# Two-block transformer kernel: opening with six shift columns as TensorE products, sums of squares moved into the joint waits

## The chip, the cores and the metric

The kernel runs on one core of one Trainium2 chip, in float32. The metric is the device time of one execution in microseconds (us), lower is better. TensorE (PE) multiplies, its weight loads are shown apart (PEld); VectorE is DVE, ScalarE is ACT, GpSimd is POOL, SyncE (SP) issues most DMAs.

## The reference

The input is one sequence of 512 tokens by 1024 features. Two blocks are computed one behind the other. What the change touches is the start of the first one and the norms:

```python
c_act = jax.nn.silu(c)
for layer in range(2):
    mod = c_act @ ada_w[layer] + ada_b[layer]            # [1024] x [1024, 6*1024]
    sh1, sc1, g1, sh2, sc2, g2 = jnp.split(mod, 6, axis=-1)
    hn = rms_norm(h, norm1_g[layer]) * (1 + sc1) + sh1
    y = recurrent_mixer(hn, ...)      # layer 0: hn @ w_in, conv, gates, scan, @ w_out
                                      # layer 1: chunk attention on keys of shared_kv
    h = h + g1 * y
    hn = rms_norm(h, norm2_g[layer]) * (1 + sc2) + sh2
    h = h + g2 * (relu(hn @ w1) ** 2 @ w2)
def rms_norm(x, g): return x * lax.rsqrt(mean(x * x, -1) + 1e-6) * g
```

The second block (two layers of three gated attention branches, an output projection with a norm behind it and a side input) follows with the same rms_norm.

## The kernel before

Features lie on partitions: `h` is 8 tiles of 128 features x 512 tokens. All weights come as a stream of "units" of 8 blocks of 128x128 (512 KB), loaded by SP into two buffers `raw`. Each unit is split in two parts, `wh` (ACT, L212) and `wl` = raw - wh (DVE, L215), and each block costs three TensorE passes of 512 columns: wl x high, wh x low, wh x high (`mm3`, L220 to L222). Activations are split the same way (`xh`, `xl`). A full unit is 24 passes. Each engine runs one in-order list; `done` and `need` are semaphore events. A unit's `wh` may be written when the unit two before it is through (same buffer).

**The opening** (L595 to L700). SP loads `crow` (the vector c on all partitions), four pairs of tiles of x, `cst` (identity and ones), `vec` (all small vectors), then 16 tiles of modulation weights, 128 features x 1024 each, in the order scale 0, shift 0, scale 1, shift 1 and so on (`early_cols`), with the first two weight units behind the fourth and the sixth. ACT squares the 8 tiles of x (L618); PE sums them over the features with eight 512-column products against `ones` (L625), once `vec` and `cst` are in; ACT takes the root (L629), DVE the reciprocal over 128x512 (L654). For tile k, DVE makes two dot products of 1024 elements with c_act (`ada_dot`, L276: scale and shift), the gain (L664) and the shift (L667) from them, and h x 1/rms (L656); ACT applies gain and shift (L674) and rounds to `xh` (L677); POOL makes `xl` (L680); PE runs the four passes on `xh` for the first two units (L511, L512) and the two on `xl` (L516). This is `first_pair`. Behind the tiles ACT makes exp and log of lambda (L682, L684), each with a table load. Then `split_first` (L528, L531) makes the first halves of units 2 and 3.

After that, the recurrent layer: per j two units (conv and gate branches), DVE taps, dots for further modulation columns, gate units. Then the out projection (L900 on): 11 units. ACT issues four loads of modulation weights ahead of it, behind the event of the last gate (`G10v`). `rounded`, `recur` and `roots_of` of tiles 8 to 10 run in its first units.

**Norms** (`rstd_of`, L431). The squares of tiles 0 to 6 are added up on DVE while the last unit still runs; in the middle of that unit, `part_sums` sums them over the partitions with four single-column products (`token_sums`, L412; a float32 product shows as two records, so 8). Behind the unit, in the wait for the last tile's square, PE runs unused passes (`idle_passes`, L406) or other work (`between`), then the sums of the last tile, then ACT's root, DVE's reciprocal of 128x4, and a product that spreads it over all partitions (L458). This stands at seven places: M0n, KV and M1n (with unused passes, `norm_mod`), twice behind the second block's output projection ("z", with two `side` products), and twice at the start of the second block's layers, where value products stand in the wait.

**Keys** (`head_sums`, L1213): the sum of squares per head of key tile j is taken by PE behind unit j + 1, except tile 0, whose sum stands ahead of unit 2.

## Time and profile before

| what | us |
|---|---|
| median of 3 runs | 2553.05 (2550.53 to 2553.19) |
| the profiled execution | 2553.41, its span 2551.6 |
| PE busy | 2490.4 (98%), 12185 passes |
| DVE, ACT, POOL busy | 1443.1, 1125.9, 43.6 |
| from the start to the first pass of unit 2 | 60.85 |

The span is the time from the first to the last instruction on the chip; what lies around it in the profiled execution is 1.8 us. Busy times of PE come from modelled ends. The granted clock is TensorE's: 1.00 is 2.4 GHz and 0.50 is 1.2 GHz.

### The profile page before, as it was taken

Reading aid. Unit: us, or ns where it says so; the run is one execution under the profiler, and the core shown is the slowest. Engines: PE = TensorE matmul, PEld = TensorE weight load, DVE = VectorE, ACT = ScalarE, POOL = GpSimd, SP = SyncE. Lnnn points to the kernel's source line nnn. Section 1 sums busy time; section 2 is a strip of 40 time slices with the busy share of each in tenths; the row PEclk is TensorE's granted clock in tenths of the full one; section 3 lists DMA queues with packets and bytes.
Section 4 is the critical chain, followed back from the end, with each engine's and each line's share of the span. In section 5 each row is a group of like instructions: output and inputs, shape, how many; then the busy total and the mean of one; then the engine's idle time right before and its main releaser. Section 6 shows DMA issues by size and latency. Waiting matters only on the chain.

```text
span 2551.6 us, 32618 instructions
## 1 busy us (share of the span) xinstructions
PE 2490.4 (98%) x12185; PEld 1974.0 (77%) x12185; DVE 1443.1 (57%) x2237; ACT 1125.9 (44%) x1993; POOL 43.6 (2%) x28
## 2 busy tenths in 40 slices
PE   5999999999999999999999999999999999999998
PEld 2887888888777688888877777778877777777887
DVE  6987655556767653433456644554465664445445
ACT  4566433433546543433445534442354544443343
POOL 2000000000000000000000000000010000000001
PEclk7999999999999999999999999999999999999999
DMA  6633466666222123222231221222322121222223
GB/s 255 233 104 132 142 204 203 209 199 216 80 91 67 44 92 106 99 99 92 98 108 66 67 67 63 78 76 91 108 82 100 67 75 60 68 77 78 91 99 107
DMA packets 77901, 280.35 MB, mean 110 GB/s; under 512 B 8640, under 2 KB 8896, under 8 KB 77504
## 3 DMA queue, kind: packets, MB, share of 16 engines
q1 hardware_dynamic: 61056, 219.60, 25.5%
q10 hardware_dynamic: 16704, 58.79, 7.0%
q8 instruction: 98, 1.61, 0.3%
q14 instruction: 43, 0.35, 0.0%
HBM read 276.26 MB, written 2.10 MB: 109 GB/s over the span
## 4 chain that ended last, share of the span: by engine, by line
PE 93%; DVE 4%; ACT 2%; issue 1%; DMA 0%; ACTq 0%; SPq 0%; DVEq 0%
PE ps L220 27%; PE ps L222 25%; PE ps L221 25%; PE ps L1784 2%; PE ps L1871 2%; PE ps L1844 1%; PE ps L1687 1%; PE ps L1788 1%; PE ps L1180 1%; PE ps L1744 1%; PE ps L1107 1%; DVE wl L215 1%; PE ps L1160 1%; ACT wh L212 1%; PE ps L1968 1%
## 5 line engine op out<-in xcount | busy, mean ns | idle before, releaser
L215 DVE TENSOR_TENSOR wl<-raw,wh 128x1024 fp32r<-128x1024 f32 x374 | 459.1, 1227 | 651.2 <-ACT wh L212 651.0
L220 PE MATMUL ps<-xh,wl 128*128 128x512 f32 x1744 | 697.9, 400 | 9.6 <-DVE wl L215 3.5
L222 PE MATMUL ps<-xh,wh 128*128 128x512 f32 x1744 | 681.9, 391 | 0.0
L221 PE MATMUL ps<-xl,wh 128*128 128x512 f32 x1744 | 681.3, 391 | 0.0
L212 ACT ACTIVATE wh<-raw 128x1024 fp32r<-128x1024 f32 x374 | 394.9, 1056 | 632.4 <-PE ps L222 620.5
L220 PE MATMUL ps<-bh,wl 128*128 128x512 f32 x1174 | 464.9, 396 | 6.4 <-DVE wl L215 2.5
L222 PE MATMUL ps<-bh,wh 128*128 128x512 f32 x1174 | 458.0, 390 | 0.0
L221 PE MATMUL ps<-bl,wh 128*128 128x512 f32 x1174 | 457.6, 390 | 0.0
L220 PEld LDWEIGHTS ps<-xh,wl 128*128 128x128 f32 x1744 | 328.3, 188 | 127.6 <-issue 45.9
L222 PEld LDWEIGHTS ps<-xh,wh 128*128 128x128 f32 x1744 | 328.4, 188 | 70.5
L221 PEld LDWEIGHTS ps<-xl,wh 128*128 128x128 f32 x1744 | 328.8, 189 | 65.8 <-issue 1.4
L220 PEld LDWEIGHTS ps<-bh,wl 128*128 128x128 f32 x1174 | 220.9, 188 | 61.6 <-DVE wl L215 5.5
L222 PEld LDWEIGHTS ps<-bh,wh 128*128 128x128 f32 x1174 | 220.7, 188 | 46.9
L221 PEld LDWEIGHTS ps<-bl,wh 128*128 128x128 f32 x1174 | 221.0, 188 | 45.1 <-issue 1.0
L1026 DVE SCALAR_TENSOR_TENSOR h<-ps,mod,h 128x512 f32<-128x512 f32 x64 | 48.0, 751 | 136.4 <-PE ps L222 136.4
L276 DVE SCALAR_TENSOR_TENSOR bA<-bA,crow 128x1024 f32<-128x1024 f32 x74 | 89.6, 1220 | 4.8 <-DMA bA<-in_ada 4.8
L1828 ACT ACTIVATE bD<-ps,sm,crow 128x128 f32<-128x128 f32 (+3 forms) x64 | 39.0, 614 | 86.9 <-DVE sm L1808 86.9
L2442 POOL TENSOR_TENSOR xl<-h,xh 128x512 fp32r<-128x512 f32 x14 | 24.9, 1792 | 2424.6 <-ACT xh L2439 2424.6
L1707 ACT ACTIVATE bD<-bD,sm 128x128 f32<-128x128 f32 (+3 forms) x64 | 36.0, 563 | 62.0 <-DVE sm L1700 61.8
L1830 ACT ACTIVATE bD<-bD,sm 128x256 f32<-128x256 f32 (+1 forms) x64 | 30.3, 475 | 74.3 <-DVE sm L1814 74.3
L1044 DVE TENSOR_TENSOR bl<-bS,bh 128x512 fp32r<-128x512 f32 x64 | 44.2, 690 | 19.8 <-ACT bh L1021 19.8
L1625 ACT ACTIVATE bT<-ps 128x512 f32<-128x512 f32 x36 | 21.5, 597 | 76.3 <-PE ps L222 76.3
(314 smaller groups left out, 2540.4 us busy)
## 6 DMA issues: line engine op xcount, KB each, us to landing
raw<-in_w SPq DMA_DIRECT2D x388, 512.0 KB, 3.3
bA<-in_ada ACTq DMA_DIRECT2D x74, 512.0 KB, 4.6
bC<-in_ada SPq DMA_DIRECT2D x9, 512.0 KB, 10.9
bD<-in_ada ACTq DMA_DIRECT2D x8, 512.0 KB, 4.3
bS<-in_attn_bias ACTq DMA_DIRECT2D x8, 512.0 KB, 3.3
bD<-in_ada SPq DMA_DIRECT2D x7, 512.0 KB, 14.8
bC<-in_ada ACTq DMA_DIRECT2D x6, 512.0 KB, 3.8
h<-in_x SPq DMA_DIRECT2D x4, 512.0 KB, 6.4
```

Source lines behind the costliest of these rows:

```text
L212: e.activation(wh[p][:], raw[p][:], ACT.Copy).then_inc(s_hi, 1)
L215: e.tensor_tensor(wl[p][:], raw[p][:], wh[p][:].bitcast(F32), ALU.subtract)\
L220: e.matmul(out, wl[p][:, blk, 0:M], xhi, start=start, stop=False)
L221: e.matmul(out, wh[p][:, blk, 0:M], xlo, start=False, stop=False)
L222: return e.matmul(out, wh[p][:, blk, 0:M], xhi, start=False, stop=stop)
L276: return e.scalar_tensor_tensor(buf, buf, 0.5, crow[:], ALU.mult, ALU.mult, accum_out=dst)
L1026: e.scalar_tensor_tensor(h[:, m, :], ps[bk][:], mod[:, g2 + m:g2 + m + 1], h[:, m, :], ALU.mult, ALU.add).then_inc(s_bank[bk], 1)
L1044: done(e.tensor_tensor(bl[:, n, :], bS[:, 2 + q, :], bh[:, n, :].bitcast(F32), ALU.subtract), f"{ev}lo{n}")
L1707: done(e.activation(x, x, ACT.Exp, bias=nm(n, m), accum_out=rs(n, m)), f"{s}{n}ex{m}")
L1784: mm = e.matmul(out[m], st["q"][m], st["k"][m], start=True, stop=not st["low"])
L1828: i = e.activation(row(n, m), ps[2 + m][:, 0:nk], ACT.Exp, bias=nm(n, m), scale=st["scale"], accum_out=rs(n, m))
L1871: mm = e.matmul(ps[6 + n // NT % 2][HD * m:HD * m + HD, at:at + P], st["v"][m][b], x[:, P * b:P * b + P], start=b == 0, stop=b == st["nk"] ...
```

## The change

In words:

1. **Sums and products of the opening.** Squares of x are added in pairs on DVE, and PE sums four pairs over the partitions with single-column products into four banks, three unused passes behind each; sixteen unused passes on zeroed data stand ahead of them. Root and reciprocal are of 4 columns and not of 512, and a product spreads them.
2. **Six of the eight shift columns** (all but tiles 3 and 6) become products on PE: eight float32 products of one column, with the modulation weights as the stationary operand (the host turns those six tiles) and c_act as a column. Products 0 and 1 stand ahead of `first_pair`; product k + 2 stands in it between the passes on `xh` and on `xl` of tile k. The scale dots stay on DVE.
3. **Engines.** Gain and shift go from DVE to ACT; `xl` and the first two `wl` go from POOL to DVE. `cst` and `vec` are loaded earlier, shift comes before scale, and the two weight units behind the second tile. Exp and log of lambda move to `decay`, in the second step of the recurrent layer.
4. **Joint waits.** `part_sums` is gone; its products stand at the head of `rstd_of`, and at M0n, KV and M1n three unused passes follow and not six.
5. **Keys.** The head sum of tile 0 stands behind unit 2, with that of tile 1.
6. **Out projection.** ACT issues the four loads in its second unit and not ahead of the first.

```diff
+DOT_TILES = (3, 6)
...
-            def part_sums(s, n, sq):
-
-                def halfway(kt):
-
-                    if pe and kt == KD // 2:
-                        need(f"{s}sp{n - 2}")
-                        done(token_sums(sq(n - 2), 6), s + "part")
-                return halfway
 
...
                 if pe:
+                    need(f"{s}sp{n - 2}")
+                    done(token_sums(sq(n - 2), 6), s + "part")
                     between[0]()
...
+            def first_pair(u0, used, s, hi, lo, tiles=range(KD), between=lambda kt: None):
...
                             e.matmul(ps[q][:], wl[p][:, kt, :], hi[:, kt, :], start=kt == 0, stop=False)
                             e.matmul(ps[q][:], wh[p][:, kt, :], hi[:, kt, :], start=False, stop=False)
+                        between(kt)
                         need(f"{s}lo{kt}")
...
-            early_cols = [c for k in range(KD) for c in (KD + k, k)]
+            early_cols = [c for k in range(KD) for c in (k, KD + k)]
...
+                e.dma_start(cst[:], io["cst"]).then_inc(s_cst, 16)
                 for i in range(4):
                     e.dma_start(h[:, 2 * i:2 * i + 2, :], io["x"][:, 2 * i:2 * i + 2, :]).then_inc(s_x[i], 16)
-                e.dma_start(cst[:], io["cst"]).then_inc(s_par, 16)
-                e.dma_start(vec[:], io["vec"]).then_inc(s_par, 16)
+                    if i == 1:
+                        e.dma_start(vec[:], io["vec"]).then_inc(s_par, 16)
                 for i, a in enumerate(early_cols):
                     if i >= ADA_SLOTS:
                         need(f"i_ada{i - ADA_SLOTS}")
                     e.dma_start(early_slots[i % ADA_SLOTS], io["ada"][a]).then_inc(s_a0[i], 16)
-                    if i in (3, 5):
-                        e.dma_start(raw[i // 2 - 1][:], io["w"][i // 2 - 1]).then_inc(s_raw[i // 2 - 1], 16)
+                    if i == 1:
+                        for q in range(2):
+                            e.dma_start(raw[q][:], io["w"][q]).then_inc(s_raw[q], 16)
...
+                need("i_zero")
+                idle_passes(16)()
+                e.wait_ge(s_cst, 16)
+                for k in range(0, KD, 2):
+                    need(f"n0sp{k}")
+                    for t in range(NT):
+                        mm = e.matmul(ps[3 + t][:, 0:1], bT[:, k, P * t:P * t + P], ones[:, 0:1], start=k == 0, stop=k == KD - 2)
+                    if k == KD - 2:
+                        done(mm, "n0sum")
+                    idle_passes(3, 7)()
...
+            def shift_product(m):
+
+                if dve and m in DOT_TILES:
+                    e.wait_ge(s_a0[2 * m], 16)
+                    done(ada_dot(early_slots[2 * m % ADA_SLOTS], sm[:, SNM + KD + m:SNM + KD + m + 1]), f"i_ada{2 * m}")
+                if pe and m < KD and m not in DOT_TILES:
+                    if m == 0:
+                        need("i_cc")
+                    if m >= 4 and m - 4 not in DOT_TILES:
+                        need(f"n0sh{m - 4}")
+                    e.wait_ge(s_a0[2 * m], 16)
+                    for kt in range(KD):
+                        mm = e.matmul(ps[2 + m % 4][:, 0:1], early_slots[2 * m % ADA_SLOTS][:, P * kt:P * kt + P], c_col[:, kt:kt + 1],
+                                      start=kt == 0, stop=kt == KD - 1)
+                    done(mm, f"i_ada{2 * m}")
+
+            if pe:
+                idle_passes(2, 6)()
+                shift_product(0)
+                idle_passes(4, 6)()
+                shift_product(1)
...
-                        done(ada_dot(early_slots[i % ADA_SLOTS], sm[:, SNM + i:SNM + i + 1]), f"i_ada{i}")
+                    shift_product(k)
+                    if k:
+                        e.wait_ge(s_a0[2 * k + 1], 16)
+                        done(ada_dot(early_slots[(2 * k + 1) % ADA_SLOTS], sm[:, SNM + k:SNM + k + 1]), f"i_ada{2 * k + 1}")
+                    if 0 < k < KD - 1:
+                        done(e.tensor_tensor(bT[:, k + 1, :], h[:, k + 1, :], ps[7][:], ALU.mult), f"n0r{k + 1}")
...
-            first_pair(0, BK, "n0", xh, xl)
+            first_pair(0, BK, "n0", xh, xl, between=lambda kt: shift_product(kt + 2))
...
-            if act:
-                need(f"G{KW - 1}v")
-                for k in range(4):
-                    ada_load(2 * KD + N_EARLY + k, out_slots[k], k)
...
+                if act and j == 1:
+                    need(f"G{KW - 1}v")
+                    for k in range(4):
+                        ada_load(2 * KD + N_EARLY + k, out_slots[k], k)
...
-                    rstd_of(s, KD, D, bTk, (idle_passes(6), idle_passes(4)), lambda: split(U[0] + 1, 0, 0))
+                    rstd_of(s, KD, D, bTk, (idle_passes(3), idle_passes(4)), lambda: split(U[0] + 1, 0, 0))
...
-                if j:
-                    head_sums(j - 1)
+                if j > 1:
+                    for m in (0, 1) if j == 2 else (j - 1,):
+                        head_sums(m)
```

## Rows read from the trace of the kernel before

**Rows 1.** The chain that ended last, shares of the span by engine.

```profile
PE 93%; DVE 4%; ACT 2%; issue 1%; DMA 0%; ACTq 0%; SPq 0%; DVEq 0%
```

**Rows 2.** Stretches: us; PE, PEld, DVE, ACT, POOL busy; clock; DMA share; GB/s.

```profile
11.88:30.20 18.32, 9.78 (x16) 3.94 (x16) 13.21 (x19) 5.48 (x8) 4.65 (x3) 0.83 1.03 412
30.20:56.00 25.80, 17.48 (x42) 10.00 (x42) 24.70 (x42) 9.50 (x14) 12.56 (x7) 0.70 0.51 193
...
70.00:100.00 30.00, 30.00 (x134) 24.71 (x133) 28.04 (x43) 15.73 (x22) 0.00 (x0) 1.00 0.71 246
```

**Rows 3.** The chain in order of time: start, us, what.

```profile
3.57 8.26 DMA vec<-in_vec
11.88 9.79 PE ps L625 x16
```

**Rows 4.** Timeline of one input tile in the opening: start, us, instruction.

```profile
44.18 1.82 POOL L680 TENSOR_TENSOR xl<-bT,xh 128x512 fp32r<-128x512 f32 x1 [2.28 <-ACT xh L677]
...
44.80 1.22 DVE L664 SCALAR_TENSOR_TENSOR gs<-sm,mod,vec 128x1 f32<-128x1 f32 x1
...
46.02 0.68 DVE L656 TENSOR_TENSOR bT<-h,bT 128x512 f32<-128x512 f32 x1
...
46.73 0.81 ACT L674 ACTIVATE bT<-bT,mod,gs 128x512 f32<-128x512 f32 x1 [2.63 <-DVE bT L656]
...
47.57 0.63 ACT L677 ACTIVATE xh<-bT 128x512 fp32r<-128x512 f32 x1
...
48.91 1.22 DVE L664 SCALAR_TENSOR_TENSOR gs<-sm,mod,vec 128x1 f32<-128x1 f32 x1
```

**Rows 5.** Timeline where the opening hands over to unit 2.

```profile
59.46 1.13 ACT L528 ACTIVATE wh<-raw 128x512 fp32r<-128x512 f32 x2
...
60.85 0.79 PE L220 MATMUL ps<-xh,wl 128*128 128x512 f32 x1 [1.46 <-DVE wl L531]
...
62.72 0.33 PEld L222 LDWEIGHTS ps<-xh,wh 128*128 128x128 f32 x1
...
65.17 0.40 PE L221 MATMUL ps<-xl,wh 128*128 128x512 f32 x1
```

**Rows 6.** Two stretches late in the kernel, around single-column products.

```profile
2051.80:2055.20 3.40, 3.24 (x31) 3.16 (x28) 1.09 (x2) 2.62 (x5) 0.00 (x0) 0.97 0.00 0
2055.20:2062.00 6.80, 5.23 (x21) 4.57 (x21) 2.39 (x9) 3.60 (x11) 0.00 (x0) 0.51 0.24 77
```

**Rows 7.** Timeline right after: products of 128 columns at the low clock.

```profile
2056.77 1.11 PE L1728 MATMUL ps<-cst,bD 128*128 128x128 f32 x4 [1.73 <-DVE bD L1720]
```

**Rows 8.** Timeline, the out projection's last unit and the first joint wait.

```profile
276.79 1.08 PEld L412 LDWEIGHTS ps<-cst,bT 128*128 128x128 f32 x8
...
282.36 1.05 PE L412 MATMUL ps<-cst,bT 128*128 128x1 f32 x8
...
284.28 1.15 PE L458 MATMUL ps<-cst,sm 128*128 128x128 f32 x8
```

**Rows 9.** Timeline, joint wait behind the second block's output projection.

```profile
1854.15 1.16 PE L458 MATMUL ps<-cst,sm 128*128 128x128 f32 x8 [0.49 <-DVE sm L453]
```

**Rows 10.** Timeline, key tiles: first head sum and unit 2.

```profile
655.73 1.13 PE L1219 MATMUL ps<-bT,cst 128*128 128x512 f32 x2 [1.53 <-ACT bT L1261]
...
656.92 0.39 PE L221 MATMUL ps<-xl,wh 128*128 128x512 f32 x1
```

**Rows 11.** Timeline at the start of the out projection.

```profile
225.92 1.06 ACT L212 ACTIVATE wh<-raw 128x1024 fp32r<-128x1024 f32 x1 [2.48 <-issue]
...
228.29 0.50 PE L220 MATMUL ps<-bh,wl 128*128 128x512 f32 x1 [2.31 <-DVE wl L215]
...
228.96 0.69 DVE L804 TENSOR_TENSOR bD<-bD,bA 128x512 f32<-128x512 f32 x1 [0.72 <-ACT bA L797]
...
233.28 1.23 DVE L215 TENSOR_TENSOR wl<-raw,wh 128x1024 fp32r<-128x1024 f32 x1 [0.26 <-ACT wh L212]
...
235.49 0.39 PE L220 MATMUL ps<-bh,wl 128*128 128x512 f32 x1
```

More of the change, by code:

```diff
@@ L498, in normed @@
                 put_lo(s, n - 1, y, shift, hi, lo)
-            def first_pair(u0, used, s, hi, lo, tiles=range(KD)):
+            def first_pair(u0, used, s, hi, lo, tiles=range(KD), between=lambda kt: None):
                 if pe:
@@ L618, in program @@
                     done(e.activation(bT[:, k, :], h[:, k, :], ACT.Square), f"n0sq{k}")
-                e.wait_ge(s_par, 32)
+                e.wait_ge(s_par, 16)
+                done(e.activation(c_th, v("c", 0, KD), ACT.Tanh, scale=0.5), "i_cth")
                 done(e.activation(sm[:, 62:63], v("eps"), ACT.Sqrt), "n0tb")
-            if pe:
-                e.wait_ge(s_par, 32)
-                for k in range(KD):
-                    need(f"n0sq{k}")
-                    mm = e.matmul(ps[7][:], ones, bT[:, k, :], start=k == 0, stop=k == KD - 1)
-                done(mm, "n0sum")
+            root = sm[:, 0:NT]
@@ L628, in program @@
                 need("n0sum")
-                done(e.activation(bT[:, 8, :], ps[7][:], ACT.Sqrt, scale=1.0 / D, bias=v("eps")), "n0root")
+                for t in range(NT):
+                    i = e.activation(root[:, t:t + 1], ps[3 + t][:, 0:1], ACT.Sqrt, scale=1.0 / D, bias=v("eps"))
+                done(i, "n0root")
+            if dve:
+                e.wait_ge(s_a0[1], 16)
+                done(ada_dot(early_slots[1], sm[:, SNM:SNM + 1]), "i_ada1")
+                need("n0root")
+                done(e.reciprocal(root, root), "n0inv")
@@ new lines, in program @@
+            if pe:
+                need("n0inv")
+                for t in range(NT):
+                    mm = e.matmul(ps[7][:, P * t:P * t + P], root[:, t:t + 1].to_broadcast([P, P]), ident, start=True, stop=True)
+                done(mm, "n0rstd")
+            def shift_product(m):
[4 more added lines that the diff above has]
+                    if m == 0:
+                        need("i_cc")
+                    if m >= 4 and m - 4 not in DOT_TILES:
[5 more added lines that the diff above has]
+                    done(mm, f"i_ada{2 * m}")
@@ L632, in program @@
                     e.activation(wh[q][:], raw[q][:], ACT.Copy).then_inc(s_hi, 1)
-            if pool:
+            if dve:
+                need("n0rstd")
+                for m in range(2):
+                    done(e.tensor_tensor(bT[:, m, :], h[:, m, :], ps[7][:], ALU.mult), f"n0r{m}")
                 for q in range(2):
@@ L679, in program @@
+                if dve:
+                    for m in (k - 1,) if 0 < k < KD - 1 else (k - 1, k) if k else ():
                         need(f"n0hi{m}")
                         done(e.tensor_tensor(xl[:, m, :], bT[:, m, :], xh[:, m, :].bitcast(F32), ALU.subtract), f"n0lo{m}")
-            if act:
-                done(e.activation(sm[:, SLAM:SLAM + KW], v("lam", 0, KW), ACT.Exp, scale=-1.0), "i_el")
-                need("i_el")
-                done(e.activation(sm[:, SLAM:SLAM + KW], sm[:, SLAM:SLAM + KW], ACT.Ln, bias=ones[:, 0:1]), "i_sp")
@@ L686, in decay @@
             def decay():
+                if act:
+                    e.wait_ge(s_cst, 16)
+                    done(e.activation(sm[:, SLAM:SLAM + KW], v("lam", 0, KW), ACT.Exp, scale=-1.0), "i_el")
+                    need("i_el")
+                    done(e.activation(sm[:, SLAM:SLAM + KW], sm[:, SLAM:SLAM + KW], ACT.Ln, bias=ones[:, 0:1]), "i_sp")
                 if dve:
@@ L985, in mlp @@
                         elif not up:
-                            unit_pe(u0, 0, i, [(bk, used, *FULL, (bh, bl))], before=by_tile(ev) if n == KD else
-                                    part_sums(nxt, KD, bTk) if c == N_FF - 1 and n == 2 * KD - 1 else None)
+                            unit_pe(u0, 0, i, [(bk, used, *FULL, (bh, bl))], before=by_tile(ev) if n == KD else None)
                         def dots():
@@ L1442, in program @@
                 elif n > 1:
-                    unit_pe(u0, 0, n, [(bk, used, *FULL, (bh, bl))], before=part_sums("M1n", KD, bTk) if n == KD - 1 else None)
+                    unit_pe(u0, 0, n, [(bk, used, *FULL, (bh, bl))])
                 if act or dve:
@@ L2467, in program @@
                     if m > 1:
-                        unit_pe(u0, 0, m, [(bk, used, *FULL, (xh, xl))],
-                                before=part_sums("L1n", KD, bDk) if l == 0 and m == KD - 1 else None)
+                        unit_pe(u0, 0, m, [(bk, used, *FULL, (xh, xl))])
                     if act:
@@ L2685, in _vectors @@
         sinks=rows(a["sw_sinks_2"]), inv_freq=freq,
-        eps=np.full((P, 1), EPS, np.float32))
+        eps=np.full((P, 1), EPS, np.float32), c=_features(a["c"][0]))
     return np.ascontiguousarray(np.concatenate([parts[k] for k in VEC], 1))
@@ L2721 @@
     ada = np.ascontiguousarray(ada.reshape(N_ADA + 2, P, D))
+    for m in range(KD):
+        if m not in DOT_TILES:
+            ada[m] = ada[m].reshape(P, KD, P).transpose(2, 1, 0).reshape(P, D)
     cst = np.zeros((P, 4, P), np.float32)
```

79 lines of the change are left out of this document (39 added, 40 removed).

## The prediction

> **What bounds the kernel now.** I read the chain of waits first, by engine [rows 1]: PE carries 93% of it, so only what PE runs, or what it waits for, counts. Then I cut the span into stretches [rows 2]. From 70 us on PE has no idle time worth the name; in 70 to 100 it is busy for all 30 us, 134 passes of 512 columns at 0.224 each, with DVE at 28.04 of 30 beside it. Before that it is not: from 30.20 to 56.00 it ran 42 passes in 25.80 us at a mean clock of 0.70, and DVE is busy 24.70 of them. So the kernel is an opening of about 61 us set by DVE, and some 2490 us of passes with a few holes.
>
> In the opening the chain [rows 3] goes through the landing of `vec` at 11.83, which PE needed for nothing but its place in the queue, then 9.79 us of sums. The timeline of a tile [rows 4] shows the period: the gain L664 of one tile starts at 44.80, of the next at 48.91, so 4.11 us a tile. In it DVE has the gain, which takes 1.22 for one column and ends where POOL's 1.82 us (44.18 to 46.00) end, 0.68 for the product with h, and in what is left, 2.2, its two dots, 1.1 each. ACT's 0.81 and 0.63 and PE's six passes fit inside. At the end [rows 5] ACT starts the halves of unit 2 only at 59.46, behind its two table loads; unit 2 starts at 60.85, with passes 0.43 apart until 65.17, when 0.227 begins. Ten passes in 4.32 us where 2.27 would do: 2.05 us lost to the clock. At the full clock unit 2 would have had the same end had it started at 62.9.
>
> **The opening, changed.** The bytes ahead of the modulation weights are the same (crow, cst, x, vec), so the last x lands where `vec` landed, near 11.8. Two squares (under 0.81 each, an L674's price) and an addition put the last pair at 13.6. Four single-column products are 8 records; in the joint wait they take 1.05, and from their start to the end of the spreading product it is 3.1 us (282.36 to 285.43) [rows 8]. The opening has four roots in place of one there, but no addition: I take the same, so 1/rms is spread at 16.7 plus up to 1 for the three extra roots and the dot of scale 0 that stands in DVE's list: 17.7. Now PE's sums alone end at 21.7 [rows 3], and its first pass waits until 30.2 [rows 2].
>
> A shift product is 16 records, 1.05 for 8, so 2.1. Two passes and product 0 end at 20.3; ACT's bias and gain (one column each, put at 0.2, between nothing and L674's 0.81), then 0.81 and 0.63 give the first high half at 22.3. Four passes and product 1 hold PE until 23.3.
> From there DVE's list is the longest: two products with h and two `wl` (1.23 each, as L215 [rows 11]) end at 21.5; then seven scale dots and two shift dots (9.9), six products with h and eight lows at 0.68 (9.5), and about 2.4 of waiting for ACT at the first and the last tile: 43.3. PE has 48 passes at 0.227 (10.9) and four products (8.4), 19.3 from 23.3: it fits under DVE by a hair. The pair of tiles k and k + 2 on PE and ACT (0.9 of passes, 2.1, then ACT's 1.9 and 0.3 of semaphores) gives 5.2 for two, 2.6 a tile: also about 43. The half of unit 2, which no table load delays now, ends 0.7 behind the last low, at 44.0. All three limits meet, so I add 1.5 for what they do to each other: unit 2 starts at 45.5, at the full clock. Modulation tiles land 1.27 apart (512 KB at 412 GB/s [rows 2]), the last near 35, five us ahead of its dot; the weight loads of units 2 and 3, behind it in SP's list, are issued near 33 and needed at 42. **Gain 62.9 - 45.5 = 17.4.**
>
> What leaves POOL costs DVE 0.7 a tile, and the gain's wait for POOL (about 1.1) goes. Exp and log come back in the second step. Tile 5 is rounded at 48.20, so tile 7 two periods on, at 56.4 [rows 4], and ACT is free again at 59.46 [rows 5]: 3.0 us with two table loads. ACT is busy 15.73 of 30 us in the next stage [rows 2], so this lies beside PE's work; DVE, which waits for it, is busy 28.04. I count nothing, and keep up to 3 us for it as a rival.
>
> **Out projection.** ACT spent 2.48 us issuing DMAs, then rounded unit 2's weights at 225.92, and PE stood 2.31 us until 228.29, then ran slow, as 7.2 us for the 24 passes to 235.49 show, where 5.45 would do [rows 11]. With the loads behind, rounding starts 2.4 earlier and this hole closes. Late next is unit 3: its `wl` hangs on root, recurrence and rounding of tile 8, from 228.96 to 234.51, 5.55 us. With the first root about 2.5 earlier it is ready at 232.0; PE would want it at 225.8 + 5.45 = 231.3, so 0.7 of waiting is left. Unit 3 started at 235.49: **gain 3.4**. The four loads (some 1.9 us of ACT's time) then lie ahead of a rounding that waits for DVE anyway, and their first dot is three units on.
>
> **Joint waits.** Taking `part_sums` out of the last unit gives back 1.08 of weight loads less the 0.19 that would stand there, 0.9 [rows 8]. At M0n, KV and M1n the six passes that fill the wait are 1.4 at 0.227; 8 records and three passes are 1.7, and DVE and ACT need about as long for the last tile's update and square: **3 x 0.9 = 2.7**. At the two z places PE is idle for only 0.49 ahead of the spreading product [rows 9], with `side` work in both gaps: I take **2 x 0.5 = 1.0**. At the two layer starts value products fill the wait already, and the sums change place only: 0. Both ends: 0 and 0.9 a place.
>
> **Keys.** PE waits 1.53 for the first head sum, and from its start to the second pass of unit 2 it is 1.19 [rows 10]. Unit 2's first half is ready, so it starts at once; the sum costs 0.9 behind it. **Gain 1.8** (the wait and what comes with it).
>
> **Sum:** 17.4 + 3.4 + 2.7 + 1.0 + 1.8 = 26.3. From the profiled 2553.41, which is 0.36 over the median: 2527.1.
>
> **A price no row shows, and the clock.** A single-column product at the low clock is not in the trace. At the full clock a record is 0.13 [rows 8]; 128-column ones at the low clock are 1.11 for four, 0.28 [rows 7]. Between them I take 0.13, as I expect the clock up after sixteen unused passes in a row: at 65.17 it rose behind ten [rows 5]. But in 2051.80 to 2055.20 PE is busy 3.24 of 3.40 us, mostly with single-column products, and the clock is 0.51 in the stretch that follows [rows 6]: such products did not hold it. The Trainium skill, "TensorE: Matmul & The Clock Gate", Part 1, says the gate follows how busy the engine has lately been, idle being the low state; read by busy time it would hold 2.4 GHz through the whole opening and leave the first rival below without a chance. The row speaks the other way, so it keeps one.
>
> **Rivals.**
> *The clock falls in the opening.* In favour: the rows just read, and the mean of 0.70 from 30.20 to 56.00. Against: the unused passes, and that DVE's list, the longest, knows no clock. A low clock over half of the pair stage makes 24 passes dearer by 0.2 (4.8) and two products by up to 2.4 each: unit 2 at 51 to 53. With 52: 2533.6. **Chance 0.22.**
> *DVE keeps the next stage.* It is busy 28.04 of 30, and PE now comes 2 us earlier against it by the better clock. If all of it is given back, with the exp and log on top of it, 3 us: 2530. Against: PE did not wait once in that stretch. **0.13.**
> *The opening gains nothing:* the clock stays low all through. Unit 2 then starts near 46 + 96r for a record price r (96 records in six products; 48 passes at 0.43 are 20.5; 22.3 + 4 for the slower start, less 3.8 counted in r; 3 of waits). At 0.13 that is 58.5; unit 2 ran slow before too, so against 60.85: gain 2.4, and 8.9 elsewhere: 2542. At 0.20 it is 65.2 and the time 2548.9. **0.04.**
> *Slower:* the same place, with the loads of the products not hidden, 0.33 each as a load at the low clock [rows 5]. Unit 2 at 77.7, 16.8 late, less 8.9: 2561.3. The point from which it decides is unit 2 at 69.8, a record price of 0.25. **0.03.**
> *My forecast:* **0.58**, 2527.1, itself within 2522 and 2531.
>
> A measurement here can tell about 0.2%, 5.1 us. Faster by more: 0.94. Same: 0.03. Slower: 0.03. The range takes in forecast, the falling clock and the next stage: 2520 to 2538; its low end is every term at its best (unit 2 at 43.4, 0.9 at all seven waits: 2522.4) and the 2.7 us by which the runs before differ, in part.
>
> **What would show it.** Unit 2's first pass at 45.5 (43.4 to 53), passes 0.227 apart there; 1/rms spread near 17.7; a period of 2.6 to 3 us in the pair; L212 of the out projection's unit 2 at its old place less 2.4 and a hole of 0.7 one unit later; no single-column records inside last units; no wait ahead of the keys' unit 2. Wrong if the granted clock is 0.50 from 20 to 45, or if a product takes over 3 us.

## The result, and the profile after

The changed kernel ran in 2537.55 us, the median of 4 runs (2536.39 to 2540.88), beside 2553.12 for the kernel before (2550.53 to 2553.43): a ratio of 0.9943, 95% interval 0.9931 to 0.9955. That is 15.6 us of the 26.3 forecast, and the profiled execution (2536.39) lies 17.0 under the profiled one of before. Run once more in a later session, the same kernel had a median of 2532.01 in 6 runs (2530.81 to 2540.88), ratio 0.9923, 0.9907 to 0.9939. By the ratios the gain is 14.6 us (11.5 to 17.6) and 19.7 us (15.6 to 23.7): the forecast of 26.3 lies outside both, though 2537.55 is still inside the range of 2520 to 2538. Both measurements belong to the result, as will be seen.

The page of the changed kernel, its head and the chain of waits by engine:

```profile
span 2534.6 us, 32918 instructions
...
PE 93%; DVE 3%; ACT 2%; issue 1%; DMA 0%; ACTq 0%; SPq 0%; DVEq 0%
```

It looks as in [rows 1]. The opening doesn't. These are its stretches, in the columns of [rows 2], one behind the other:

```profile
9.10:12.40 3.30, 2.99 (x21) 2.41 (x20) 1.62 (x3) 2.56 (x6) 0.00 (x0) 1.00 1.01 395
12.50:22.70 10.20, 10.20 (x39) 9.08 (x38) 3.49 (x11) 5.10 (x11) 0.00 (x0) 0.50 1.02 413
22.80:26.10 3.30, 3.30 (x27) 3.12 (x27) 3.30 (x4) 1.36 (x4) 0.00 (x0) 1.00 1.02 405
26.20:36.30 10.10, 10.10 (x38) 9.04 (x38) 7.84 (x15) 5.18 (x12) 0.00 (x0) 0.50 1.00 400
36.40:46.00 9.60, 9.25 (x59) 7.95 (x58) 8.31 (x15) 6.25 (x13) 0.00 (x0) 1.00 0.59 222
```

PE is busy 10.20 of 10.20 us at a granted clock of 0.50 (1.2 GHz), has 3.30 us at 1.00 (2.4 GHz), and then 10.10 at 0.50 again. What that did to single instructions, in the timeline of PE (start, duration; L646 is a sum, L408 an unused pass, L663 the spreading, L678 a shift product, L506 at 27.95 the first pass of the pair, L222 unit 2):

```profile
14.06 1.70 PE L646 MATMUL ps<-cst,bT 128*128 128x1 f32 x8
15.62 1.63 PE L408 MATMUL ps<-bh 128*128 128x512 f32 x3
17.05 1.70 PE L646 MATMUL ps<-cst,bT 128*128 128x1 f32 x8
...
20.03 1.91 PE L663 MATMUL ps<-cst,sm 128*128 128x128 f32 x8
...
27.95 0.77 PE L506 MATMUL ps<-xh,wl 128*128 128x512 f32 x1
...
29.81 3.41 PE L678 MATMUL ps<-mod,bC 128*128 128x1 f32 x16
...
51.38 0.40 PE L222 MATMUL ps<-xh,wl 128*128 128x512 f32 x1
```

A sum is 1.70 where eight records had been 1.05 [rows 8], the three passes behind it 1.63 (0.94 at the full clock), and the last sum starts at 17.05 although its squares were added at 14.1. A product at the low clock is 3.41, 0.21 a record: the price no row had shown, between my ends of 0.13 and 0.28. Unit 2 starts at 51.38, not at 45.5.

Here is the same kernel, same instructions, in the execution profiled later:

```profile
12.50:22.70 10.20, 9.98 (x73) 8.98 (x73) 7.41 (x16) 7.41 (x15) 0.00 (x0) 1.00 1.03 413
...
26.20:36.30 10.10, 9.77 (x53) 8.27 (x52) 10.10 (x17) 6.20 (x13) 0.00 (x0) 0.83 1.03 409
```

```profile
14.74 0.95 PE L646 MATMUL ps<-cst,bT 128*128 128x1 f32 x8
...
16.71 1.16 PE L663 MATMUL ps<-cst,sm 128*128 128x128 f32 x8 [0.22 <-DVE sm L659]
...
22.59 0.47 PE L506 MATMUL ps<-xh,wl 128*128 128x512 f32 x1
...
23.60 1.84 PE L678 MATMUL ps<-mod,bC 128*128 128x1 f32 x16
...
45.26 0.40 PE L222 MATMUL ps<-xh,wl 128*128 128x512 f32 x1
```

The same 10.2 us held 73 records in place of 39, 1/rms was spread at 17.87 (forecast 17.7; 21.94 in the first trace), and unit 2 started at 45.26 (forecast 45.5). So unit 2 starts at 45 or at 51 us by what the clock does ahead of it, and 5.4 of the 6.1 us between the two are there before the pair begins (22.59 and 27.95). The times differ in the same way: ten executions of this kernel fall in two groups, four of 2530.8 to 2532.4 at mean clocks of 0.994 and 0.995, six of 2536.4 to 2540.9 at 0.989 to 0.992. The first measurement had four of the second group. One execution of each group was traced, 2530.81 and 2536.39; that the other eight had one of these two openings is likely, but no trace shows it.

**Where the time went, place by place.** I matched PE's passes of a trace with those of the kernel before in their order, and took the lead (start before less start after) on both sides of each place. For example, unit 2 of the out projection starts at 228.29 [rows 11] and at 216.52: a lead of 11.8.

| place (start before, us) | forecast | after | after, 2nd execution |
|---|---|---|---|
| opening (to 66) | 17.4 | 11.5 | 17.6 |
| next stage (66 to 100) | 0 | -2.2 | -2.2 |
| out projection (225 to 245) | 3.4 | 3.3 | 3.3 |
| joint wait M0n (270 to 290) | 0.9 | 0.6 | 0.6 |
| KV (625 to 645) | 0.9 | 0.9 | 1.0 |
| keys (655 to 670) | 1.8 | 1.8 | 1.8 |
| M1n (915 to 935) | 0.9 | 1.0 | 1.0 |
| layer start (1270 to 1290) | 0 | 0.1 | 0.1 |
| z (1840 to 1860) | 0.5 | 0.9 | 1.0 |
| layer start (1900 to 1950) | 0 | 1.0 | 0.9 |
| z (2475 to 2495) | 0.5 | 0.9 | 0.9 |
| clock elsewhere, and rest | 0 | -2.9 | -3.2 |
| **sum** | **26.3** | **17.0** | **22.8** |

The last line but one is a net figure: the kernel before has falls of its own in these stretches.

The next stage's rows (after): DVE goes from one instruction to the next without a break, and PE waits for its `wl`.

```profile
75.61 1.21 DVE L278 SCALAR_TENSOR_TENSOR bC<-bC,crow 128x1024 f32<-128x1024 f32 x1
...
76.75 1.22 DVE L217 TENSOR_TENSOR wl<-raw,wh 128x1024 fp32r<-128x1024 f32 x1
```

```profile
62.79 0.50 PE L222 MATMUL ps<-xh,wl 128*128 128x512 f32 x1 [0.33 <-DVE wl L217]
78.03 0.50 PE L222 MATMUL ps<-xh,wl 128*128 128x512 f32 x1 [1.34 <-DVE wl L217]
```

```profile
70.00:100.00 30.00, 28.66 (x127) 23.40 (x126) 28.50 (x43) 18.77 (x26) 0.00 (x0) 1.00 0.78 264
```

PE has 127 passes where it had 134 [rows 2]. DVE's first step of the stage is 9.2 us earlier than before (52.73 for 61.91) and its list was as long, so 9.2 is what PE can keep of its 11.5; in the second execution 15.4 of 17.6.

Out projection, unit 2 and the unit behind it (beside [rows 11]):

```profile
216.52 0.46 PE L222 MATMUL ps<-bh,wl 128*128 128x512 f32 x1
...
222.69 0.50 PE L222 MATMUL ps<-bh,wl 128*128 128x512 f32 x1 [0.48 <-DVE wl L217]
```

The hole of 2.31 is gone, and one of 0.48 (forecast 0.7) has come one unit later. The first joint wait (beside [rows 8]):

```profile
267.10 0.95 PE L414 MATMUL ps<-cst,bT 128*128 128x1 f32 x8
...
268.77 1.05 PE L414 MATMUL ps<-cst,bT 128*128 128x1 f32 x8
...
271.04 1.16 PE L453 MATMUL ps<-cst,sm 128*128 128x128 f32 x8 [0.18 <-DVE sm L448]
```

And a place where the clock fell in this trace but not in the one of before:

```profile
735.00:746.00 11.00, 9.83 (x45) 7.00 (x45) 7.69 (x16) 5.79 (x14) 0.00 (x0) 0.84 0.32 109
```

The stretch 751 to 762 of before has the same work at 1.00; here 1.5 us go. (In the traces of `best1`, `best2` and both with dots it did not fall there.) The next fall that the kernel before did not have, at 1852, takes the lead from 16.2 to 13.6. Behind 2495 it is the kernel before that loses more, and 1.2 come back. The second layer start brings 1.0 that I had put at 0, for a reason that stood in the trace of before and that I had not read: inside that last unit PE waited for the sum of squares.

```profile
1908.92 1.05 PE L412 MATMUL ps<-cst,bD 128*128 128x1 f32 x8 [0.82 <-DVE bD L399]
```

### The profile page after: what moved, and what is told of

The parts are those of the page before. It is cut to its first block, busy times and chain, and to the rows that moved or that the text cites. A ratio compares the mean times of both kernels' runs of the same rounds, so it can differ in the third digit from the quotient of the medians.

```text
span 2534.6 us, 32918 instructions
## 1 busy us (share of the span) xinstructions
PE 2503.8 (99%) x12330; PEld 1996.8 (79%) x12330; DVE 1433.1 (57%) x2225; ACT 1131.5 (45%) x2013; POOL 25.0 (1%) x18
## 4 chain that ended last, share of the span: by engine, by line
PE 93%; DVE 3%; ACT 2%; issue 1%; DMA 0%; ACTq 0%; SPq 0%; DVEq 0%
PE ps L222 26%; PE ps L224 25%; PE ps L223 25%; PE ps L1831 2%; PE ps L1918 2%; PE ps L1891 1%; PE ps L1734 1%; PE ps L1835 1%; DVE wl L217 1%; PE ps L1226 1%; PE ps L1791 1%; PE ps L1153 1%; ACT wh L214 1%; PE ps L1206 1%; PE ps L408 1%
## 5 line engine op out<-in xcount | busy, mean ns | idle before, releaser
L222 PE MATMUL ps<-xh,wl 128*128 128x512 f32 x1744 | 698.2, 400 | 9.8 <-DVE wl L217 5.2
L222 PE MATMUL ps<-bh,wl 128*128 128x512 f32 x1174 | 463.7, 395 | 4.4 <-DVE bl L1388 2.0
L222 PEld LDWEIGHTS ps<-xh,wl 128*128 128x128 f32 x1744 | 328.5, 188 | 127.7 <-issue 45.4
L222 PEld LDWEIGHTS ps<-bh,wl 128*128 128x128 f32 x1174 | 220.5, 188 | 59.9 <-issue 4.8
L1090 DVE TENSOR_TENSOR bl<-bS,bh 128x512 fp32r<-128x512 f32 x64 | 44.2, 690 | 19.8 <-ACT bh L1067 19.8
L1171 ACT ACTIVATE bA<-bA,sm 128x128 f32<-128x128 f32 (+3 forms) x64 | 36.0, 563 | 38.3 <-DVE sm L1165 35.0
```

The lines of the kernel that those rows point to most:

```text
L222: e.matmul(out, wl[p][:, blk, 0:M], xhi, start=start, stop=False)
L1090: done(e.tensor_tensor(bl[:, n, :], bS[:, 2 + q, :], bh[:, n, :].bitcast(F32), ALU.subtract), f"{ev}lo{n}")
```

## The experiments

The question: why 15.6 and not 26.3, and is it the clock, DVE's list or the products? Each kernel ran beside the kernel before, whose own 31 executions in these sessions were 2549.92 to 2557.27, so times are compared by ratio; a mean clock is rounded to 0.001, which is 2.5 us in one execution. "Work" below is the mean of time x granted clock, "clock" the rest of the mean time. It tells executions of one kernel apart; between kernels it is only a hint, as a low clock while PE waits is in it. Two ratios whose intervals overlap are not told apart by these times.

| kernel | ratio to before (95%) | median | lowest, highest | work + clock |
|---|---|---|---|---|
| changed, 10 executions | 0.9943 and 0.9923 | 2536.5 | 2530.8, 2540.9 | 2516.2 + 19.8 |
| opening_only | 0.9958 (0.9943 to 0.9972) | 2542.6 | 2538.7, 2547.7 | 2525.6 + 17.4 |
| later_only | 0.9961 (0.9948 to 0.9974) | 2545.1 | 2541.6, 2546.8 | 2518.4 + 26.0 |
| more_passes | 0.9920 (0.9907 to 0.9932) | 2533.6 | 2531.1, 2536.0 | 2521.3 + 12.2 |
| none_between | 0.9927 (0.9914 to 0.9941) | 2532.9 | 2530.8, 2539.8 | 2514.2 + 20.3 |
| dots_all | 0.9911 (0.9897 to 0.9924) | 2531.4 | 2528.8, 2536.8 | 2518.5 + 14.2 |
| dots_again | 0.9932 (0.9919 to 0.9945) | 2536.1 | 2533.1, 2541.8 | 2517.4 + 19.3 |
| short_dots | 0.9902 (0.9887 to 0.9917) | 2528.2 | 2527.2, 2533.3 | 2514.0 + 15.2 |
| best1 | 0.9909 (0.9893 to 0.9924) | 2530.6 | 2528.6, 2532.6 | 2515.4 + 15.2 |
| best2 | 0.9907 (0.9892 to 0.9922) | 2528.8 | 2527.5, 2534.6 | 2516.7 + 13.3 |
| best3 | 0.9897 (0.9883 to 0.9911) | 2528.7 | 2528.2, 2529.2 | 2518.0 + 10.7 |

**The opening alone, and the rest alone.** `later_only` is the kernel before with the places behind the opening changed, as in the cut below; `opening_only` is the changed kernel with all of them put back:

```diff
                 if pe:
+                    need(f"{s}sp{n - 2}")
+                    done(token_sums(sq(n - 2), 6), s + "part")
                     between[0]()
...
-                        if m == KD - 1:
-                            part_sums("M0n", KD, bTk)(kt - 3)
...
+                if act and j == 1:
+                    need(f"G{KW - 1}v")
+                    for k in range(4):
+                        ada_load(2 * KD + N_EARLY + k, out_slots[k], k)
...
-                    rstd_of(s, KD, D, bTk, (idle_passes(6), idle_passes(4)), lambda: split(U[0] + 1, 0, 0))
+                    rstd_of(s, KD, D, bTk, (idle_passes(3), idle_passes(4)), lambda: split(U[0] + 1, 0, 0))
...
-                if j:
-                    head_sums(j - 1)
+                if j > 1:
+                    for m in (0, 1) if j == 2 else (j - 1,):
+                        head_sums(m)
```

> The changed opening with all later parts as before. Ledger of the two traces: unit 2 of the first stage is 11.4 us earlier, of which 9.4 are left from 88 us on, when DVE has kept the next stage. So 2553.1 - 9.4 = 2543.7. Rival (the loss of 2 us in the next stage has nothing to do with the opening): 2541.7. Rival (opening as forecast, 17.4, and the trace of after was an unlucky one): 2535.7.

> The opening as before, the out projection's loads, the sums in the joint waits and the keys' head sum as changed. Ledger of the traces by place: 3.4 + 0.4 + 0.9 + 1.8 + 1.0 + about 0 at the layer starts and the z places = 7.5, so 2545.6. By the forecast's terms 8.9: 2544.2. Rival (the lead after the opening is what lets these gains come through, DVE would keep them otherwise): under 5, above 2548.

2542.6 and 2545.1, 10.0 and 7.5 under the 2552.6 of the kernel before beside them: both first theories, within 1.1 us. By the ratios they are 10.7 and 10.0, each within some 3.5 us, so the times alone show only roughly that the parts add up. The traces show more. In that of `later_only` the places of its theory give 3.3, 0.9, 1.0, 1.8 and 1.0, in the whole change 3.3, 0.6, 0.9, 1.8 and 1.0. But the z places and the second layer start, which the theory had at about 0, give 2.8 more, and falls of the clock elsewhere take back some 4 of the 10.9: that the median met 7.5 is luck. In that of `opening_only` unit 2 starts at 51.96, the next stage returns 2.2, and two places that it leaves alone move: the out projection gives 0.8, as a fall of the clock that the kernel before has at 229 us is missing, and M0n gives -0.35. So M0n leans on the opening: DVE's addition there starts 0.46 us behind the end of the last sum in every trace with tile 0's shift column as a product, and 0.10 behind it in every other. The reason stays open.

**More unused passes, and none between the sums.** `more_passes` and `none_between` against the changed kernel:

```diff
-                    idle_passes(3, 7)()
+                    idle_passes(6, 7)()
...
-                idle_passes(2, 6)()
+                idle_passes(6, 6)()
...
-                idle_passes(4, 6)()
+                idle_passes(8, 6)()
...
-            between=lambda kt: shift_product(kt + 2)
+            between=lambda kt: (idle_passes(4 if kt == 0 else 0, 6)(), shift_product(kt + 2))
```

```diff
-                    idle_passes(3, 7)()
+                    if k == KD - 2:
+                        idle_passes(3, 7)()
```

> Changed kernel with six unused passes behind each sum in place of three, six ahead of product 0 in place of two, eight between products 0 and 1 in place of four, and four ahead of product 2. Theory A (the clock set the opening's miss): the granted clock stays up from its first rise on, products 1.84 in place of 2.7 and 3.4, unit 2's first pass near 47 in place of 51.4, the time 2 to 4 us under the changed kernel's (the next stage returns up to half). Theory B (DVE's list and the order of the pair set it): unit 2 at 51 to 52 even with the clock up, no gain. If the clock falls all the same: unit 2 at 53 or later, slower than the changed kernel by 1 to 3.

> Changed kernel without the unused passes behind the first three sums (three stay behind the last). In the trace of after they did not hold the clock and stood in the sums' way, 1.63 us for three at the low clock. Theory A1 (they only cost): the last sum starts at 14.2 in place of 17.05, 1/rms is spread near 19.5 in place of 21.9, unit 2 near 49.5, time down by 1.5 to 2.5. Theory A2 (they give back what they cost, as the clock stays low longer without them): last sum at 14.2 all the same, but the low clock lasts through more of the pair and unit 2 comes at 51 to 54, time the same or up to 2 us more.

`more_passes`: the clock stayed up through the sums and the first four products and fell later in the pair. Its stretches and two instructions:

```profile
12.00:20.00 8.00, 8.00 (x50) 7.07 (x50) 3.14 (x10) 4.93 (x11) 0.00 (x0) 1.00 1.03 415
...
36.00:46.00 10.00, 10.00 (x38) 8.65 (x36) 6.71 (x11) 4.79 (x10) 0.00 (x0) 0.53 0.72 270
```

```profile
36.81 3.41 PE L678 MATMUL ps<-mod,bA 128*128 128x1 f32 x16
...
50.98 0.40 PE L222 MATMUL ps<-xh,wl 128*128 128x512 f32 x1
```

So A held only for the sums: unit 2 at 50.98 in this execution. The added passes have a price of their own, as the pair's first pass came at 25.80, 3.2 later than in the second execution of the changed kernel, with the clock up in both. Yet the highest of its five times is 2536.0, where six of the changed kernel's ten are above that. Its work is 5 us dearer, its clock 8 cheaper. `none_between` is the other way round: the last sum starts at 14.80, unit 2 at 49.55, A1 in this trace; its times lie in two groups (four of 2530.8 to 2533.8, two of 2539.2 and 2539.8), so A2 may be what two of the six executions did; no trace shows those.

**Products or dots.** All eight shift columns on DVE:

```diff
-DOT_TILES = (3, 6)
+DOT_TILES = tuple(range(8))
```

> Changed kernel with all eight shift columns as DVE dots (no product at all; the rest of the opening as changed). Products took 14.2 us of PE in the trace of after between 22.6 and 47.6; six dots are 6 x 1.22 more for DVE. Theory A (PE is the longest of the pair as the clock is low in it, DVE has room of about 3 us): DVE's list from 22 is 31 us, unit 2 at 53 to 54, time 2 to 3 us over the changed kernel's ratio. Theory B (DVE was the longest already): unit 2 at 58 to 59, 7 us over. If products were a loss: unit 2 before 51.4.

Unit 2 started at 53.36, the 53 to 54 of theory A, and PE waited for DVE's low halves once in each of five tiles, four times for 1.43 us:

```profile
47.51 0.73 PE L512 MATMUL ps<-xl,wh 128*128 128x512 f32 x2 [1.43 <-DVE xl L729]
...
53.36 0.39 PE L222 MATMUL ps<-xh,wl 128*128 128x512 f32 x1
```

But its median was 2531.4, 6 under the changed kernel's first one, against every theory. Before making a story of it I ran both kernels in turn on one chip.

> The changed kernel once more, beside two others. In the runs so far the time of an execution times its mean granted clock is nearly constant for one kernel (changed: 2515.9 with a spread of 0.4 in four runs; before: 2528.8), and what differs is what the clock takes: 20 to 25 us. Theory A (the clock falls at other places from one execution to the next, the work is the same): time times clock again 2515 to 2517, times between 2530 and 2541. Theory B (the changed kernel has a fixed clock pattern, two falls of 10 us in the opening each time): times within 2536 to 2541 as before, clock 0.990 to 0.992 in each.

> The kernel with all eight shift columns as dots once more, on the same chip and in turn with the changed one. If the products are what the clock falls over (theory A), it is faster than the changed kernel in the same session by 3 us or more, with a mean clock of 0.993 to 0.996, though its unit 2 starts 2 us later at the same clock. If its 2531.4 was only what the clock happened to do in five executions (theory B): within 2 us of the changed kernel, or slower by up to 2.

2532.0 for the changed kernel, 2536.1 for the dots. Theory A for the first, though time times clock went from 2512.6 to 2518.2 in single executions, beyond its band by more than the rounding of the clock. The second is not faster, so its theory A is out; it is slower by 4.1 by the medians and by 2.3 by the ratios, where B had up to 2. The 2531.4 was what five executions happened to give. At a low clock over the sums in all three, unit 2 starts at 53.4 and 53.7 with dots and at 51.4 with products: in the traces the six products are worth 2 us or a little more, as the low clock lasted to 36.4 us there and to 33.2 and 33.3 with dots. The times don't show that: the ratios overlap, and over ten executions each the means are 2534.7 with dots and 2535.9 with products.

**DVE in the next stage.**

```diff
-            def ada_dot(buf, dst):
-
-                return e.scalar_tensor_tensor(buf, buf, 0.5, crow[:], ALU.mult, ALU.mult, accum_out=dst)
+            def ada_dot(buf, dst, w=2 * T):
+
+                return e.scalar_tensor_tensor(buf[:, 0:w], buf[:, 0:w], 0.5, crow[:, 0:w], ALU.mult, ALU.mult, accum_out=dst)
...
-                        done(ada_dot(conv_slots[k], mod[:, 2 * KD + t:2 * KD + t + 1]), f"g1ada{t}")
+                        done(ada_dot(conv_slots[k], mod[:, 2 * KD + t:2 * KD + t + 1], 64 if t < 6 else 2 * T), f"g1ada{t}")
```

> Changed kernel with the first six modulation dots of the next stage over 64 columns in place of 1024 (their outputs are then other ones; it leaves out 6 x 1.1 us of DVE). Theory A (DVE keeps the next stage, and so returns 2 of the 11.4 us): PE's waits of 0.33 at 62.8 and 1.34 at 78.0 go, the lead on before stays at 11 us or more, time down by 1.7 to 2. Rival (the waits come from ACT's order, its exp, log and loads ahead of the rounding): the waits stay, no change.

This kernel leaves out most of six dots, so its output is another one; it serves for its times alone.

```profile
71.19 0.43 PE L222 MATMUL ps<-xh,wl 128*128 128x512 f32 x1
```

This is the pass that waited 1.34 at 78.03; it waits for nothing now, though PE is earlier (unit 2 at 46.69). The lead over before is 16.2 at 66 us and 16.2 at 100 us: nothing is returned. In the changed kernel PE's waits there were 1.7 us, and 2.2 were returned. Theory A. The time, 2528.2, has the lowest work of all kernels, 2514.0. The opening is that of the changed kernel, and the clock in it took a third course:

```profile
12.00:20.00 8.00, 7.78 (x55) 6.92 (x56) 5.16 (x12) 5.51 (x12) 0.00 (x0) 1.00 1.03 415
20.00:26.00 6.00, 6.00 (x30) 5.47 (x29) 5.97 (x10) 3.84 (x8) 0.00 (x0) 0.64 1.03 408
26.00:36.00 10.00, 10.00 (x47) 8.81 (x47) 7.77 (x14) 5.10 (x11) 0.00 (x0) 0.70 1.02 405
```

It was up over the sums and low over the start of the pair, and unit 2 was only 1.4 us later than at its best.

**Six passes kept in the joint waits.**

```diff
-                    rstd_of(s, KD, D, bTk, (idle_passes(3), idle_passes(4)), lambda: split(U[0] + 1, 0, 0))
+                    rstd_of(s, KD, D, bTk, (idle_passes(6), idle_passes(4)), lambda: split(U[0] + 1, 0, 0))
```

> Changed kernel with six unused passes in the joint waits as in the kernel before, in place of three. Read at the places alone, from the lead over the kernel before ahead of the sums to that behind the spreading product: 0.44 at the first, 0.94 and 1.0 at the next two in the changed kernel. If the three passes taken out are what was gained: 0.7 less at each of the three. If DVE's and ACT's work for the last tile sets the wait: no difference, and the gain is that of the records alone.

By the leads: 0.1, 0.5 and 0.5 at M0n, KV and M1n in place of 0.6, 0.9 and 1.0. So about 0.5 of each gain is the three passes, where the first theory had 0.7, and the rest is the records. This is one execution; in the other traces KV and M1n are 0.9 to 1.0 throughout, M0n is 0.6 in the five with tile 0's shift column as a product and 0.9 to 1.0 in the other six.

**Another opening.** The diff is that of `best1`, but for its last two lines: these are what `best2` adds to it, three passes behind each product in the pair but tile 7's; `best3` has 38, 6 and 12 unused passes for 32, 5 and 5, and column 1 among the dots, so that product 1 goes.

```diff
-DOT_TILES = (3, 6)
+DOT_TILES = (0, 3, 6)
...
+                    if k in (2, 4):
+                        need(f"n0sp{k}")
+                        done(e.tensor_tensor(bT[:, k, :], bT[:, k, :], bT[:, k - 2, :], ALU.add), f"n0st{k}")
+                        need(f"n0st{k}")
...
-                idle_passes(16)()
+                idle_passes(32)()
...
-                for k in range(0, KD, 2):
+                for k in (4, 6):
...
-                    idle_passes(3, 7)()
+                    if k == KD - 2:
+                        idle_passes(5, 7)()
...
+                e.wait_ge(s_a0[0], 16)
+                done(ada_dot(early_slots[0], sm[:, SNM + KD:SNM + KD + 1]), "i_ada0")
+                need("n0root")
+                done(e.reciprocal(root, root), "n0inv")
...
-                idle_passes(2, 6)()
-                shift_product(0)
-                idle_passes(4, 6)()
-                shift_product(1)
+                idle_passes(5, 6)()
+                shift_product(1)
...
-            between=lambda kt: shift_product(kt + 2)
+            between=lambda kt: (shift_product(kt + 2), idle_passes(3 if kt + 2 < KD and kt + 2 not in DOT_TILES else 0, 6)())
```

> Changed kernel with another opening: squares of tiles 0 to 5 added up on DVE, so two sums in place of four; 32 unused passes ahead of them, none between, five behind; shift column 0 as a DVE dot ahead of the reciprocal, the scale column 0 behind it; product 1 alone ahead of the pair. Spread near 16.5 to 17.5 in place of 21.9, first pass of the pair near 20.5 in place of 27.95. Then DVE's list of 23 us: unit 2 at 44 to 46 if the clock stays up, and the lead of the first conv step over before grows by as much: 2531. If the clock falls in the pair, as it did with products and passes alone: unit 2 at 48, 2534. Rival (the modulation tiles' landing or DVE's next stage keeps it all): 2537.

> As best1, with three unused passes behind each of the three products in the pair that come before tile 7's, and that one. They cost 0.7 each on PE. Theory A (the clock falls in the pair because of the products, and passes behind them hold it): no low stretch before unit 2, unit 2 at 43.5 to 45.5, at or under best1's time. Rival (PE's order is the longest even at the full clock, the passes only cost): unit 2 up to 2.5 us later than best1's.

> As best2, with shift column 1 as a DVE dot too, so that nothing but 512-column passes, one pair of sums and the spreading product runs ahead of the pair: 38 unused passes ahead of the sums, six behind, twelve behind the spreading. DVE's list is longer by 1.2 us. Theory A (holding the clock is worth more than a dot): clock up from its first rise to the end of the opening, unit 2 at 45 to 46.5, mean clock 0.996, time 2527 to 2529. Rival (DVE's list sets the pair once the clock is up): unit 2 at 47 or later, 2530 or more.

```profile
45.31 0.51 PE L222 MATMUL ps<-xh,wl 128*128 128x512 f32 x1 [1.15 <-DVE wl L527]
```

```profile
24.56 3.41 PE L685 MATMUL ps<-mod,bC 128*128 128x1 f32 x16
...
47.62 0.39 PE L222 MATMUL ps<-xh,wl 128*128 128x512 f32 x1
```

The first is `best1`, the second `best2`. Both medians lie under both of the changed kernel's, but their ratios overlap with its second one. In both traces the clock fell once behind the sums and once in the pair, and `best1` came out at its forecast of 2531 all the same. In `best2` it fell before its first three passes behind a product (24 to 31 us), so passes behind products were not tested there; unit 2 was 2.3 later than in `best1`, as its rival had it, but with the clock low for longer, so that this decides nothing between the two. In `best3` it did not fall in the opening, nor until 732 us:

```profile
9.00:45.00 36.00, 34.46 (x191) 28.46 (x190) 31.15 (x54) 24.87 (x50) 0.00 (x0) 1.00 0.97 389
```

```profile
23.57 1.84 PE L685 MATMUL ps<-mod,bC 128*128 128x1 f32 x16
...
45.10 0.50 PE L222 MATMUL ps<-xh,wl 128*128 128x512 f32 x1
```

Its four times lie within 1.0 us of each other, where every other kernel that was run more than once spread over 4 to 10. Theory A: 2528.7, the lowest ratio of the table, 3.3 under the changed kernel's median in the same session and 9 under the first measurement; its interval just overlaps with that of the changed kernel's second one. Its lowest time is within 1.1 us of those of `short_dots`, `best1` and `best2`; what it didn't have, in four executions, are long ones. It differs from `best2` in three counts of passes and in product 1, so which of them kept the clock up is open, and so is whether four executions are enough to say that it stays up.

## Why the prediction was wrong

**The parts, with the clock up over the sums, were right.** In the second execution, where the clock fell only for short stretches in the pair, the opening gave 17.6 (17.4), the out projection 3.3 (3.4), the keys 1.8 (1.8), the five joint waits 4.4 (3.7). The spread 1/rms, unit 2's start and the new hole of the out projection came within 0.3 us. Of the seven waits, M0n was put too high (0.6 for 0.9, by 0.35 that the changed opening costs there), both z too low (0.9 for 0.5), and the second layer start gave 1.0 where I had said 0; without the next stage the places of this execution sum to 28.2, for 26.3.

**First step that failed: the forecast took the sum of every term at a clock that holds, and priced its fall as a rival of 0.22.** "I expect the clock up after sixteen unused passes in a row." It is up by their end, from 9.1 on, but it does not hold: it is at 0.50 from 12.5 and again from 26.2, the opening's term of 17.4 measured 11.5, and six executions of ten took 7.5 us more than the other four (means of 2539.0 and 2531.4). Five traces have this very opening: two of the changed kernel, `opening_only`, `short_dots` and `six_kept`. In two the clock fell over the sums (at 12.5 and 13.2 us): 1/rms was spread at 21.9 and 22.5, unit 2 started at 51.4 and 52.0, and the gain at 66 us was 11.5 and 10.9. In three it fell later (at 21.7, 22.0 and 30.6): 1/rms at 17.7 to 17.9, unit 2 at 45.3 to 46.9, the gain 16.0 to 17.6. So it is a low clock over the sums that costs. The rival had unit 2 at 51 to 53, and it came at 51.38, but that is in good part luck: I had put the loss in the pair, where even the low stretch of `short_dots` cost only 1.4 us. Over the sums it costs twice, as the unused passes stand in the sums' way, 1.63 us for three. The row that I had read against the change, PE busy 3.24 of 3.40 us with single-column products and then 0.51 [rows 6], was the better witness than the three unused passes between.

The Trainium skill, "TensorE: Matmul & The Clock Gate", Part 1, has the gate follow how busy the engine has been. Read by the busy time of the profile, the traces here don't agree: in 12.50 to 22.70 PE was busy for all 10.20 us at 0.50, and in the other execution for 9.98 at 1.00; and in the two stretches ahead of the falls, 9.10 to 12.40 and 22.80 to 26.10, it was busy 2.99 and 3.30 of 3.30 us at 1.00. `best3`, with 38 passes in a row and passes behind its products, is the only opening in which no fall was seen.

**Second step that failed: the next stage, "I count nothing".** The rival of 0.13, priced at 3 us, came every time: 2.1 to 2.4 us are returned in every trace of a changed opening with the dots at full length, and none in `short_dots`. The rows had it: DVE at 28.04 of 30 beside a PE that did not wait once [rows 2]. What I argued from, that PE did not wait, was true only while PE was as late as DVE; the 2.05 us that the better clock gives unit 2 are PE's alone, and DVE returns just these. The exp and log cost nothing on top: `short_dots` has them too and returns nothing.

**Third: rivals that can hold together were given as alternatives.** The clock and DVE's list both took their part, and with a net 2.9 us for the clock outside the opening (falls at 740 and 1852 us of the trace above all; I had counted none) the sum for the profiled run is 26.3 - 5.9 (opening) - 2.2 (next stage) - 2.9 (clock elsewhere) + 1.7 (the small places) = 17.0. The range reached to 2538 and held six of the ten executions of the changed kernel (2530.8 to 2536.6); it lacked what one kernel's executions differ by, 10 us.

**The other rivals.** The clock low all through, or a product's records above 0.25: neither; records are 0.21 at the low clock, and the clock was never low from 20 to 45 without a break. No run tests their tipping points. Of the two signs of being wrong that I had named, one came: a product took over 3 us (3.41 at 29.81). It is no special price of a product, only the low clock.

What stays open: why the clock falls over the sums in one execution and not in the next, with the same instructions. In the first it rose at about 9, in the second at about 7, but that does not sort them: of the five traces with this opening it rose first in that of `opening_only`, at 6.4, and fell over the sums there. Nor was it tried to hold the clock at 740 or 1850.

## What to carry to other kernels

Where PE's work is thin, first ask in how many executions the clock holds: compare the granted clocks of several runs, not of one profile, since the same kernel may differ by 10 us. Then ask where a low clock would lie on the path: over a chain that everything waits for (here the sums) it cost 4 to 5 us, over a stretch that DVE's list covers 1 to 2. If such a chain depends on it, cover it with 512-column passes while PE waits for others anyway, and keep single-column products out of it: in `best3`, the kernel that went furthest in this, the long executions were missing. Passes where PE does not wait cost what they take. And when PE gets ahead, look for the engine that was exactly as late: what it can't follow is given back at its next long list.

## What the runs showed of the hardware

- Single-column products: 16 records take 1.84 us at a clock of 1.00 and 3.41 at 0.50; eight take 0.95 and 1.70.
- From the start, PE's first unused passes came 0.42 us apart (the sixteen take 6.68 us from 3.09), while the stretch 4 to 9 is shown with a clock of 1.00; 0.23 came only from 6 to 9 us on. A clock of 1.00 ahead of its first change in a trace says nothing.
- The unused passes began at 3.08 to 3.09 in every trace that has them ahead of the sums (3.1 us of issue), although the memset that they wait for ended at 1.94.
- Two medians of five executions of one kernel, in two sessions on two chips, differed by 4.7 us (2531.4 and 2536.1), more than most of the effects looked for here.
- The clock fell at other places of the opening from one execution to the next, with the same instructions: at 12.5 and 26.1 us in one trace of the changed kernel, at 30.6 and 40.8 in the other. Near 740 us it fell in nine of the thirteen traces of kernels with a change, and not in that of the kernel before.
